# Residual projections taken by column halves, and the weight splits, banks and convolution parts that follow, in a two-block transformer kernel

## The chip, the cores and the metric

The kernel runs on one core of a Trainium2 chip. The metric is the device time of one execution in microseconds (us), the median of three runs. Smaller is better. TensorE (PE) multiplies, VectorE (DVE), ScalarE (ACT) and GpSimd (POOL) work elementwise, SyncE (SP) issues the transfers.

## The reference, cut to what matters

256 tokens of width 1024 pass through two blocks. The first has four token mixers and an MLP with squared ReLU; the second has block attention with rotary embedding, a causal depthwise convolution of 31 taps, and a gated MLP. Both blocks share one skeleton, in which the changed code lies:

```python
h = rms_norm(x, mix_norm_g)
ys, gate_logit = _token_mixers(h, w_in, ...)
x = x + jnp.sum(gates * branch, axis=2) @ w_out       # "wo"
h = rms_norm(x, mlp_norm_g)
x = x + jnp.square(jax.nn.relu(h @ w_up)) @ w_down    # "up", "dn"
x = rms_norm(x, final_norm_g)
h = rms_norm_2(x, norm1_g)
proj = h @ w_in_2                                     # "p2": q, k, v, u
attn = moba_attention(rope(norm(q)), rope(norm(k)), v)
conv = conformer_conv(u, glu_b, dw_w, dw_b, ln_g, ln_b)
x = x + jnp.concatenate([attn, conv], axis=-1) @ w_out_2   # "wo2"
h = rms_norm_2(x, norm2_g)
x = x + (silu(h @ w_gate) * (h @ w_up_2)) @ w_down_2       # "g", "u", "d2"
```

## The kernel before

**Products.** Every large product is made in float32 precision by three passes of rounded operands: a weight `w` becomes `whi` (rounded, a cast on ScalarE, `split_hi`, L998) and `wlo = w - whi` (VectorE, `split_lo`, L1403), and an activation likewise `Ahi/Alo`, `Bhi/Blo`, `hhi/hlo` (L1012, L1417). `product` (L536 to L538) multiplies hi by hi, hi by lo and lo by hi for up to four blocks of 128 rows, so a product of 512 columns is 12 matmuls. A product is named by a tag such as `("up", j, ui, t)`: `t` is the half of the tokens (0 or 1), `ui` the half of the contraction, `n` the half of the output columns.

**Weight units.** Weights arrive in units of 1 MB (512 rows by 512 columns). Each unit serves two products, one for each `t`. SyncE loads units into four `raw` buffers; a load waits until both splits of the unit four before are done. The split results live in three slots (`NSPL = 3`), so unit i may be split only when the last product of unit i-3 is done.

**Order.** There is no scheduler at run time: each engine has a fixed list, and semaphores hold it where it must wait. TensorE's order of products is `groups`. ScalarE and VectorE call `after(tag)` and `before(tag)` at the place of each product in their own lists; these issue the split of unit i+2 at the last product of unit i (`ends`). Whatever stands behind a waiting instruction in a list waits too.

**The joints.** Where a residual is followed by a normalisation, the order is special. The last four products of "wo", "dn" and "wo2" go (t, n) = (0,0), (0,1), (1,0), (1,1). Each adds to the residual `xr` on VectorE (`residual`, L1659), is transposed by TensorE (`turn_res`, into bank 5+n), scaled by the gain (`gained`, `x_gain` L1423) and split (L1012, L1417); ScalarE squares it (L1151) for the norm. The first chunk of the next stage goes in `FIRST` order, (ui, t) = (0,0), (1,0), (0,1), (1,1), and all later chunks in `PLAIN` order, (0,0), (0,1), (1,0), (1,1). `W_ACC` gives the accumulators of (t, n): banks 3, 4, 7, 0. The first chunks of "p2" use banks 0 and 1, so the first one waits for the residual that empties bank 0.

**Behind "p2".** Each chunk of "p2" is evacuated by `evac2` (L1248), which for the first chunk waits for two inverse roots (`stats2`: four squares "F" of `xr` times a gain that GpSimd multiplies in at L1972). Then come the rotary work (`r0`, `ra`, `r1` on VectorE, L1764 to L1793, turned by `rturn`), and a loop over ten steps k with eight attention heads (`az` scores, `at` transposition, `ap` times V, `aw` evacuation at L1293/L1294), between which TensorE makes 16 parts of the convolution (`conv`, L845), two in each of the first eight steps. `ln_turn`, `ln`, `ln_back` and `ln_silu` are the convolution's LayerNorm and swish, placed among the first four "wo2" products.

Of the kernel before, what the change touches and what calls it, by code (L numbers as in the profile page):

```python
# [17 lines left out]
NPC = 2  # L18
# [53 lines left out]


# [90 lines left out]
def build(nc, ctx, x_d, w_in, w_br, w_out, w_up, w_dn, w_in2, w_out2, w_g2, w_u2, w_d2, par_d, par2_d, cst_d, tw_d, out_d):  # L164
# [143 lines left out]
    def plan_out(name, src):  # L308
# [4 lines left out]
        for t in range(2):  # L313
            for n in range(2):
                group(u[1][n], name, 1, n, t)

    def plan_down(name, src, j, kn, last):
        if kn == 4:
            u = [add_unit(src, 4 * j, 4, 512 * n, 512) for n in range(2)]
            for n, t in ([(n, t) for t in range(2) for n in range(2)] if last else PLAIN):  # L320
                group(u[n], name, j, n, t)
# [5 lines left out]
    def plan_up(name, src, j, n, first):  # L327
        u = [add_unit(src, 4 * k, 4, 512 * j, n) for k in range(2)]
        for ui, t in (FIRST if first else PLAIN):
            group(u[ui], name, j, ui, t)  # L330

    plan_out("wo", w_out)
    for j in range(8):
        plan_up("up", w_up, j, 512, j == 0)
        if j:
            plan_down("dn", w_dn, j - 1, 4, False)
    plan_down("dn", w_dn, 7, 4, True)
    for i, (c0, n) in enumerate(CH2):
        u = [add_unit(w_in2, 4 * k, 4, c0, n) for k in range(2)]
        for ui, t in (FIRST if i == 0 else PLAIN):  # L340
            group(u[ui], "p2", i, ui, t)
    plan_out("wo2", w_out2)
    for j in range(6):
        plan_up("g", w_g2, j, HC2[j] * 128, j == 0)
        plan_up("u", w_u2, j, HC2[j] * 128, False)
        if j:
            plan_down("d2", w_d2, j - 1, HC2[j - 1], False)
    plan_down("d2", w_d2, 5, 2, True)

    nu = len(units)  # L350

    free_at = {}
    ends = {}
    for tag, i in unit_of.items():
        free_at[i] = groups[tag] + 1
    for i, g in free_at.items():
        ends[g - 1] = i
# [10 lines left out]
    for key in [("A", t, h) for t in range(2) for h in range(2)] + [("B", t, h) for h in range(2) for t in range(2)] \  # L368
            + [("M", t, h) for h in range(2) for t in range(2)] + [("N1", t, n) for t in range(2) for n in range(2)] \
            + [("H", j, t) for j in range(8) for t in range(2)] + [("N2", t, n) for t in range(2) for n in range(2)] \  # L370
            + [("Y", t, h) for h in range(3) for t in range(2)] + [("N3", t, n) for t in range(2) for n in range(2)] \
# [7 lines left out]
    SQ = {key: i for i, key in enumerate([("x", t) for t in range(2)] + [(k, t, n) for k in ("N1",) for t in range(2)  # L379
                                                                       for n in range(2)]  # L380
                                         + [("N2", t, n) for t in range(2) for n in range(2)]
                                         + [("F", t, n) for t in range(2) for n in range(2)]
                                         + [("N3", t, n) for t in range(2) for n in range(2)])}
# [110 lines left out]
    def _(e):  # L494
# [261 lines left out]
        def turn_res(name, t, n):  # L756
            key = (name, t, n)
            base = {"N1": 0, "N2": 4, "N3": 8}[name]
            w.wait_ge(s_res, base + 2 * t + n + 1)
# [13 lines left out]
        for t in range(2):  # L773
            for n in range(2):
                bk = W_ACC[t, n]
                w.wait_ge(s_xl, X["M", t, 1] + 1)
                product(("wo", 1, n, t), Ahi, Alo, 4, t, lambda c0, bk=bk: bank[bk], False, True)
                gone[bk] = (s_res, 2 * t + n + 1)
                if (t, n) != (0, 0):
                    turn_res("N1", *((0, 0), (0, 1), (1, 0))[2 * t + n - 1])  # L780

        def up(name, j, src, hi, lo, first, tail=None):
            for q, (ui, t) in enumerate(FIRST if first else PLAIN):
# [9 lines left out]
        def down(name, j, key, last, tail=None):  # L793
            hi, lo = hhi[:, j % 2], hlo[:, j % 2]
            for k, (n, t) in enumerate([(n, t) for t in range(2) for n in range(2)] if last else PLAIN):
# [5 lines left out]
                if last:  # L801
                    gone[bk] = (s_res, 4 + 2 * t + n + 1)
# [6 lines left out]
        for j in range(8):  # L809
            up("up", j, "N1", Bhi, Blo, j == 0, (lambda: turn_res("N1", 1, 1)) if j == 0 else None)  # L810
# [6 lines left out]
        down("dn", 7, "H", True, lambda k: k and turn_res("N2", *((0, 0), (0, 1), (1, 0))[k - 1]))  # L817
# [53 lines left out]
        def ap(h):  # L871
            w.wait_ge(s_ev, 36 + 10)
            w.wait_ge(s_ac, h + 1)
            clear(2)
            P, v = PT2[:, h % 2, :], V2[:, :, 64 * h:64 * h + 64]
            e.matmul(bank[2][:, 0:64], P[:, 0:128], v[:, 0, :], start=True, stop=True)
            e.matmul(bank[2][:, 64:128], P[:, 128:256], v[:, 0, :], start=True, stop=False)
            e.matmul(bank[2][:, 64:128], P[:, 256:384], v[:, 1, :], start=False, stop=True).then_inc(s_ap, 1)
            gone[2] = (s_aw, h + 1)
# [21 lines left out]
        gone[0], gone[1] = (s_ev, 45), (s_ev, 46)  # L901
        for k in range(10):
            if k < 8:
                az(k)
                conv(2 * k)
            if 1 <= k < 9:
                at(k - 1)
            if k < 8:
                conv(2 * k + 1)
            if k > 1:  # L910
                ap(k - 2)
        for t in range(2):
# [3 lines left out]
            turn_x(key, ys[:, t, 0:512])  # L916

# [32 lines left out]
        for t in range(2):  # L950
            for n in range(2):
                bk = W_ACC[t, n]
                product(("wo2", 1, n, t), Bhi, Blo, 4, t, lambda c0, bk=bk: bank[bk], False, True,
                        at={0: (s_xl, X["Y", t, 1] + 1), 2: (s_xl, X["Y", t, 2] + 1)})
                gone[bk] = (s_res, 8 + 2 * t + n + 1)
                if (t, n) != (0, 0):
                    turn_res("N3", *((0, 0), (0, 1), (1, 0))[2 * t + n - 1])


        for j in range(6):  # L960
            nk = HC2[j]
            up("g", j, "N3", Ahi, Alo, j == 0, (lambda: turn_res("N3", 1, 1)) if j == 0 else None)
            gone[1], gone[2] = (s_sg, 2 * j + 1), (s_sg, 2 * j + 2)
            up("u", j, None, Ahi, Alo, False)
# [13 lines left out]
    def _(e):  # L978
# [175 lines left out]
        def norm_turn(name, t, n, o):  # L1154
            base = {"N1": 0, "N3": 8}[name]
            w.wait_ge(s_res, base + 2 * t + n + 1)
# [12 lines left out]
        def out_proj(name, norm, o):  # L1169
# [8 lines left out]
            for t in range(2):  # L1178
                for n in range(2):
                    after(name, 1, n, t)  # L1180
                    if (t, n) != (0, 0):
                        p = ((0, 0), (0, 1), (1, 0))[2 * t + n - 1]
                        norm_turn(norm, *p, o)
                        gained((norm, *p))

        out_proj("wo", "N1", o2)

        def plain_order(first):
            return FIRST if first else PLAIN
# [12 lines left out]
        for j in range(8):  # L1202
            for q, (ui, t) in enumerate(plain_order(j == 0)):
                after("up", j, ui, t)
# [3 lines left out]
                if q == (2 if j == 0 else 3):  # L1208
                    relu2(j, 0)
            if j:  # L1210
                for k, (n, t) in enumerate(PLAIN):
                    after("dn", j - 1, n, t)
# [866 lines left out]
```

## Time and profile before

| | |
|---|---|
| median of 3 runs | 847.89 us (847.79 to 848.2) |
| the profiled execution | 847.93 us |
| its span, first to last instruction | 846.1 us |
| TensorE busy | 807.1 us (95%) |
| VectorE, ScalarE, GpSimd busy | 467.6, 406.5, 33.9 us |
| mean granted TensorE clock | 0.991 |

The span is the time from the first to the last recorded instruction; about 1.8 us of the execution lie outside it. TensorE's matmuls overlap: a record of 0.39 us starts every 0.227 us, so the end that the profile draws lies 0.16 us behind the start of what may follow. An idle time in brackets is counted from that drawn end.

### The profile page before, as it was taken

The page shows a single profiled execution, that of the slowest core. Times are in us where ns is not written, and L with a number is a line of the kernel's source. Part 1 is how long each engine was busy: PE and PEld are TensorE (multiplying, and loading weights), DVE is VectorE, ACT ScalarE, POOL GpSimd, SP SyncE. Part 2 cuts the span into 40 slices and gives each one's busy share as a digit, 9 for nine tenths or more (in the row PEclk, how much of TensorE's full clock was granted, in tenths as well). Part 3 has the DMA queues.
Part 4 walks back from the last instruction along what each step waited for, and adds up shares of the span by engine and source line. Part 5 has one row for each costly group of instructions (what it writes and reads, how often), then busy time and mean ns, then how long its engine had stood idle before and what let it go on. Part 6 is the DMA issues. An engine that isn't in the chain of part 4 may idle for free.

```text
span 846.1 us, 9700 instructions
## 1 busy us (share of the span) xinstructions
PE 807.1 (95%) x3930; PEld 663.6 (78%) x3930; DVE 467.6 (55%) x616; ACT 406.5 (48%) x539; POOL 33.9 (4%) x33
## 2 busy tenths in 40 slices
PE   6999999999999898999999998999998999999997
PEld 4887888877778686888888876877876788888896
DVE  5445354556756865454444447688735555444543
ACT  6554454454546626555454436454435443344341
POOL 0000000000000410000000003020000000000000
PEclk9999999999999999999999999999989999999999
DMA  9742424333446364555555546644112654654441
GB/s 336 284 150 76 149 75 149 119 138 142 147 153 195 110 225 151 197 173 181 195 193 184 177 144 241 214 149 149 51 49 71 229 184 142 224 196 149 140 159 50
DMA packets 68268, 136.25 MB, mean 161 GB/s; under 512 B 2304, under 2 KB 7040, under 8 KB 67584
## 3 DMA queue, kind: packets, MB, share of 16 engines
q1 hardware_dynamic: 67760, 134.44, 46.5%
q10 hardware_dynamic: 464, 1.20, 0.4%
q8 instruction: 31, 0.51, 0.2%
q14 instruction: 13, 0.11, 0.0%
HBM read 134.43 MB, written 1.05 MB: 160 GB/s over the span
## 4 chain that ended last, share of the span: by engine, by line
PE 87%; DVE 6%; ACT 3%; issue 2%; POOL 1%; DMA 1%; ACTq 0%; SPq 0%; DVEq 0%
PE b L536 19%; PE b L538 18%; PE b L537 18%; PE SS L536 4%; PE SS L538 4%; PE SS L537 4%; PE TT L505 3%; DVE wlo L1403 2%; PE OO L536 2%; PE OO L537 2%; PE OO L538 2%; PE OO L845 2%; PE SS L621 1%; PE b L680 1%; DMA xr<-in_x 1%
## 5 line engine op out<-in xcount | busy, mean ns | idle before, releaser
L1403 DVE TENSOR_TENSOR wlo<-raw,whi 128x2048 fp32r<-128x2048 f32 (+2 forms) x123 | 271.7, 2217 | 103.6 <-ACT whi L998 103.6
L998 ACT CAST whi<-raw 128x2048 fp32r<-128x2048 f32 (+2 forms) x123 | 227.5, 1850 | 124.5 <-PE b L538 93.2
L536 PE MATMUL b<-whi,Ahi 128*128 128x512 f32 (+2 forms) x568 | 222.2, 391 | 9.0 <-DVE wlo L1403 3.7
L538 PE MATMUL b<-whi,Alo 128*128 128x512 f32 (+2 forms) x568 | 216.1, 381 | 0.0
L537 PE MATMUL b<-wlo,Ahi 128*128 128x512 f32 (+2 forms) x568 | 215.5, 379 | 0.0
L536 PEld LDWEIGHTS b<-whi,Ahi 128*128 128x128 f32 x568 | 107.7, 190 | 32.3 <-issue 8.1
L538 PEld LDWEIGHTS b<-whi,Alo 128*128 128x128 f32 x568 | 107.4, 189 | 20.9
L537 PEld LDWEIGHTS b<-wlo,Ahi 128*128 128x128 f32 x568 | 107.9, 190 | 18.4
L536 PE MATMUL b<-whi,Bhi 128*128 128x512 f32 x168 | 66.7, 397 | 5.5 <-DVE wlo L1403 2.8
L1417 DVE TENSOR_TENSOR hlo<-TT,hhi 128x512 fp32r<-128x512 f32 (+1 forms) x28 | 17.7, 668 | 91.3 <-ACT hhi L1012 91.3
L538 PE MATMUL b<-whi,Blo 128*128 128x512 f32 x168 | 65.5, 390 | 0.0
L537 PE MATMUL b<-wlo,Bhi 128*128 128x512 f32 x168 | 65.5, 390 | 0.0
L536 PE MATMUL SS<-whi,hhi 128*128 128x512 f32 x108 | 42.4, 392 | 1.7 <-DVE hlo L1417 1.7
L1012 ACT CAST hhi<-TT 128x512 fp32r<-128x512 f32 (+1 forms) x28 | 14.8, 573 | 57.8 <-PE TT L505 57.8
L538 PE MATMUL SS<-whi,hlo 128*128 128x512 f32 x108 | 42.1, 389 | 0.0
L537 PE MATMUL SS<-wlo,hhi 128*128 128x512 f32 x108 | 42.0, 389 | 0.0
L536 PEld LDWEIGHTS b<-whi,Bhi 128*128 128x128 f32 x168 | 31.5, 188 | 12.7 <-DVE gates L1640 3.4
L538 PEld LDWEIGHTS b<-whi,Blo 128*128 128x128 f32 x168 | 31.5, 188 | 6.7
L537 PEld LDWEIGHTS b<-wlo,Bhi 128*128 128x128 f32 x168 | 31.6, 188 | 6.1
L1947 POOL TENSOR_TENSOR st<-st 128x2 f32<-128x2 f32 (+3 forms) x13 | 15.4, 1183 | 414.6 <-DVE st L1427 414.6
L1084 ACT ACTIVATE Sb<-Sb,st 128x384 f32<-128x384 f32 (+3 forms) x16 | 9.9, 617 | 39.2 <-DVE st L1522 39.2
L536 PEld LDWEIGHTS SS<-whi,hhi 128*128 128x128 f32 x108 | 20.3, 188 | 6.3 <-DVE hlo L1417 2.2
(264 smaller groups left out, 999.7 us busy)
## 6 DMA issues: line engine op xcount, KB each, us to landing
raw<-in_w_in SPq DMA_DIRECT2D x42, 1024.0 KB, 4.9
raw<-in_w_up SPq DMA_DIRECT2D x16, 1024.0 KB, 5.4
raw<-in_w_dn SPq DMA_DIRECT2D x16, 1024.0 KB, 7.2
raw<-in_w_d SPq DMA_DIRECT2D x11, 1024.0 KB, 5.0
raw<-in_w_g SPq DMA_DIRECT2D x10, 1024.0 KB, 5.3
raw<-in_w_u SPq DMA_DIRECT2D x10, 1024.0 KB, 4.9
raw<-in_w_out SPq DMA_DIRECT2D x8, 1024.0 KB, 5.0
raw<-in_w_br SPq DMA_DIRECT2D x4, 1024.0 KB, 5.1
```

Source lines behind the costliest of these rows:

```text
L505: ins = e.transpose(dst[:, 128 * k:128 * k + 128], src[:, 128 * k:128 * k + 128], ident)
L536: e.matmul(dst, xh, H[:, kc, c0:ce], start=first and kc == krs[0], stop=False)
L537: e.matmul(dst, xh, L[:, kc, c0:ce], start=False, stop=False)
L538: ins = e.matmul(dst, xl, H[:, kc, c0:ce], start=False, stop=last and kc == krs[-1])
L621: ins = e.matmul(SS[:, m * g:m * g + m], qkA[p:p + 64, q, qs], qkA[p:p + 64, k, 0:m], start=True, stop=True)
L845: ins = e.matmul(bank[7][:, 128 * i:128 * i + 128], tw[:, i % 3, 128 * j:128 * j + 128], hp[:, i, j:j + 128], start=j == 0, stop=j == NSH - 1)
L998: e.copy(whi[:, s, 0:m], raw[:, r, 0:m]).then_inc(s_hi, 1)
L1012: e.copy(ph, src).then_inc(s_xh, 1)
L1084: ins = e.activation(P, P, ACT.Exp, bias=stat_m[i][:, 0:1], accum_out=stat_s[i][:, 0:1])
L1403: e.tensor_tensor(wlo[:, s, 0:m], raw[:, r, 0:m], whi[:, s, 0:m].bitcast(F32), ALU.subtract).then_inc(s_lo, 1)
L1417: e.tensor_tensor(pl, src, ph.bitcast(F32), ALU.subtract).then_inc(s_xl, 1)
L1947: e.tensor_tensor(r, v, mhalf[:, 0:n], ALU.pow).then_inc(s_rs, 1)
```

## The change

All four-product ends of residual projections go by column halves: `ORD` gives (t, n) = (0,0), (1,0), (0,1), (1,1), so that a weight unit's two products are neighbours. The first chunks of "up", "p2" and "g" go in `PLAIN` order as all others. The turned residuals go to bank 5+t. "p2" uses banks 1 and 2 in place of 0 and 1, and `ap` bank 0 in place of 2. From the first residual's last four products on, unit i is split at the place of the product just behind the last one of unit i-3, one place earlier than before; up to there the places stay. At the joints, calls of `after` and `before` now stand behind the residual's and the gain's work. The convolution's parts are spread otherwise over the attention loop: two in steps 0 to 3, one in steps 4 to 9, one behind the loop and one behind the turns of the attention's result.

```diff
+ORD = [(0, 0), (1, 0), (0, 1), (1, 1)]
...
-    bg[2] += [("gt", 0)]
-    bg[3] += [("gs", 0)]
-    bg[4] += [("gt", 1)]
+    bg[3] += [("gt", 0)]
+    bg[4] += [("gs", 0), ("gt", 1)]
...
+    turn = groups["wo", 1, 0, 0]
+    split_after = {}
+    for i in range(NPC, nu):
+        g = free_at[i - 2] - 1
+        if g >= turn:
+            g = free_at[i - NSPL]
+        assert g not in split_after, (g, i)
+        split_after[g] = i
...
-        xbank[key] = {"A": (3 if a else 5) + n, "M": 5 + a, "N1": 5 + n, "N2": 5 + n, "N3": 5 + n, "H": 5 + n,
+        xbank[key] = {"A": (3 if a else 5) + n, "M": 5 + a, "N1": 5 + a, "N2": 5 + a, "N3": 5 + a, "H": 5 + n,
...
-            clear(2)
+            clear(0)
...
-        gone[0], gone[1] = gone[W_ACC[1, 1]], (s_up, 15)
         for i in range(5):
-            for q, (ui, t) in enumerate(FIRST if i == 0 else PLAIN):
+            for q, (ui, t) in enumerate(PLAIN):
                 w.wait_ge(s_xl, X["N2", t, ui] + 1)
                 if ui == 0 and i == 0:
-                    clear(t)
+                    clear(1 + t)
...
-                product(("p2", i, ui, t), Ahi, Alo, 4 * ui, t, lambda c0, t=t: bank[t], ui == 0, ui == 1)
+                product(("p2", i, ui, t), Ahi, Alo, 4 * ui, t, lambda c0, t=t: bank[1 + t], ui == 0, ui == 1)
...
         for k in range(10):
             if k < 8:
                 az(k)
-                conv(2 * k)
+                tile_part()
             if 1 <= k < 9:
                 at(k - 1)
-            if k < 8:
-                conv(2 * k + 1)
+            if k < 4 or k > 7:
+                tile_part()
             if k > 1:
                 ap(k - 2)
+        tile_part()
...
+        tile_part()
...
-            i = ends.get(groups[tag])
-            if i is not None and i + 2 < nu:
-                split_hi(i + 2)
+            if groups[tag] in split_after:
+                split_hi(split_after[groups[tag]])
...
-            i = ends.get(groups[tag] - 1)
-            if i is not None and i + 2 < nu:
-                split_lo(i + 2)
+            i = split_after.get(groups[tag] - 1)
+            if i is not None and i > split_done[0]:
+                split_lo(i)
+                split_done[0] = i
...
-                if q == (2 if i == 0 else 3):
+                if q == 3:
                     evac2(i, 0)
+                after("p2", i, ui, t)
...
-            for t in range(2):
-                for n in range(2):
-                    before(name, 1, n, t)
-                    w.wait_ge(s_mm, done(name, 1, n, t))
-                    residual(base, t, n)
-                    if (t, n) != (0, 0):
-                        p = ((0, 0), (0, 1), (1, 0))[2 * t + n - 1]
-                        gained((norm, *p), pcol(gain, 4 * p[1], 4))
+            for k, (t, n) in enumerate(ORD):
+                w.wait_ge(s_mm, done(name, 1, n, t))
+                residual(base, t, n)
+                if k:
+                    p = ORD[k - 1]
+                    gained((norm, *p), pcol(gain, 4 * p[1], 4))
+                before(name, 1, n, t)
```

## Rows read from the trace of the kernel before

**Rows 1.** The page: busy time, share of the span, instructions of TensorE
```profile
PE 807.1 (95%) x3930; PEld 663.6 (78%) x3930; DVE 467.6 (55%) x616; ACT 406.5 (48%) x539; POOL 33.9 (4%) x33
```
**Rows 2.** Waits of TensorE: us in total, times, longest
```profile
PE b L536 <- DVE wlo L1403: 6.5, 6, 1.4
```
**Rows 3.** Timeline of TensorE, first residual into "up": start, us, what [idle before]
```profile
323.39 0.47 PE L536 MATMUL b<-whi,Bhi 128*128 128x512 f32 x1 [1.42 <-DVE wlo L1403]
...
328.17 0.47 PE L536 MATMUL b<-whi,Bhi 128*128 128x512 f32 x1 [1.33 <-DVE wlo L1403]
...
338.01 0.66 PE L505 MATMUL TT<-cst,ust 128*128 128x128 f32 x4 [1.00 <-ACT ust L1200]
```
**Rows 4.** The page's costliest groups: the two splits; busy, mean ns | idle before
```profile
L1403 DVE TENSOR_TENSOR wlo<-raw,whi 128x2048 fp32r<-128x2048 f32 (+2 forms) x123 | 271.7, 2217 | 103.6 <-ACT whi L998 103.6
L998 ACT CAST whi<-raw 128x2048 fp32r<-128x2048 f32 (+2 forms) x123 | 227.5, 1850 | 124.5 <-PE b L538 93.2
```
**Rows 5.** Timeline of TensorE from the second residual into "p2"
```profile
513.40 0.47 PE L536 MATMUL b<-whi,Ahi 128*128 128x512 f32 x1 [2.39 <-DVE xr L1659]
...
525.38 0.66 PE L505 MATMUL TT<-cst,ys 128*128 128x128 f32 x4 [1.49 <-ACT ys L1248]
...
528.62 0.39 PE L536 MATMUL b<-whi,Ahi 128*128 128x512 f32 x1
```
**Rows 6.** Stretches: us, busy of PE, PEld, DVE, ACT, POOL, PEclk, DMA share, GB/s
```profile
513.40:518.17 4.77, 4.77 (x16) 3.81 (x17) 3.39 (x3) 1.24 (x3) 0.43 (x1) 0.64 0.73 220
...
617.57:623.21 5.64, 5.64 (x14) 4.37 (x15) 1.14 (x2) 2.89 (x2) 0.00 (x0) 0.51 0.00 0
...
700.34:711.22 10.88, 10.88 (x49) 8.96 (x48) 3.38 (x3) 3.82 (x2) 0.00 (x0) 1.00 0.58 193
```
**Rows 7.** Timeline of ScalarE: the first evacuation of "p2"
```profile
524.64 0.69 ACT L1248 ACTIVATE ys<-b,st 128x512 f32<-128x512 f32 x1 [0.51 <-DVE st L1759]
```
**Rows 8.** Timelines of VectorE and GpSimd where both read SBUF
```profile
509.39 1.11 DVE L1417 TENSOR_TENSOR Alo<-tg,Ahi 128x512 fp32r<-128x512 f32 x1 [0.69 <-ACT Ahi L1012]
...
511.87 1.97 POOL L1972 TENSOR_TENSOR xr<-xr,par 128x512 f32<-128x512 f32 x1 [1.92 <-ACT ys L1151]
...
518.56 1.30 POOL L1972 TENSOR_TENSOR xr<-xr,par 128x512 f32<-128x512 f32 x1 [4.73 <-PE TT L505]
```
**Rows 9.** The rotary stretch, columns as in rows 6
```profile
549.10:578.59 29.49, 27.44 (x125) 21.55 (x124) 25.86 (x39) 16.89 (x20) 8.06 (x4) 1.00 0.46 153
```
**Rows 10.** Timeline of TensorE: the third turn of the rotary work
```profile
574.06 0.66 PE L505 MATMUL TT<-cst,PT 128*128 128x128 f32 x4 [0.39 <-DVE PT L1793]
```
**Rows 11.** Timelines in the attention loop: convolution parts, taps on VectorE
```profile
604.51 1.11 PE L845 MATMUL OO<-hp,tw 128*128 128x128 f32 x8
...
608.85 1.10 PE L845 MATMUL OO<-hp,tw 128*128 128x128 f32 x8
...
600.99 2.84 DVE L1831 SCALAR_TENSOR_TENSOR ca<-ch,par,ca 128x256 f32<-128x256 f32 x7
```
**Rows 12.** Timeline of TensorE: the loop's end into "wo2"
```profile
614.04 0.41 PE L876 MATMUL b<-V,PT 128*128 128x64 f32 x2 [0.70 <-ACT ys L1294]
...
615.51 1.25 PE L505 MATMUL TT<-cst,ys 128*128 128x128 f32 x8 [0.61 <-ACT ys L1294]
...
617.57 0.79 PE L536 MATMUL SS<-whi,Bhi 128*128 128x512 f32 x1 [0.81 <-DVE Blo L1417]
```
**Rows 13.** Timeline of TensorE: the third residual into "g" and "u"
```profile
640.32 0.79 PE L536 MATMUL OO<-whi,Bhi 128*128 128x512 f32 x1 [2.32 <-DVE wlo L1403]
...
653.12 0.47 PE L536 MATMUL b<-whi,Ahi 128*128 128x512 f32 x1 [1.41 <-DVE wlo L1403]
...
657.89 0.47 PE L536 MATMUL b<-whi,Ahi 128*128 128x512 f32 x1 [1.33 <-DVE wlo L1403]
...
666.14 0.39 PE L536 MATMUL b<-whi,Ahi 128*128 128x512 f32 x1
```
**Rows 14.** DMA issues: count, KB each, median us to landing
```profile
raw<-in_w_dn SPq DMA_DIRECT2D x16, 1024.0 KB, 7.2
```

More of the change, by code:

```diff
@@ L312, in plan_out, with plan_down @@
                 group(u[0][n], name, 0, n, t)
-        for t in range(2):
-            for n in range(2):
-                group(u[1][n], name, 1, n, t)
-    def plan_down(name, src, j, kn, last):
+        for n, t in PLAIN:
+            group(u[1][n], name, 1, n, t)
+    def plan_down(name, src, j, kn):
         if kn == 4:
             u = [add_unit(src, 4 * j, 4, 512 * n, 512) for n in range(2)]
-            for n, t in ([(n, t) for t in range(2) for n in range(2)] if last else PLAIN):
+            for n, t in PLAIN:
                 group(u[n], name, j, n, t)
@@ L325, in plan_down, with plan_up @@
                 group(u, name, j, 0, t)
-    def plan_up(name, src, j, n, first):
+    def plan_up(name, src, j, n):
         u = [add_unit(src, 4 * k, 4, 512 * j, n) for k in range(2)]
-        for ui, t in (FIRST if first else PLAIN):
+        for ui, t in PLAIN:
             group(u[ui], name, j, ui, t)
@@ L772, in _, with up @@
                         turn_x(("M", t_, 1), ys[:, t_, 512:1024])
[L773 to L778, printed above, removed]
-                if (t, n) != (0, 0):
-                    turn_res("N1", *((0, 0), (0, 1), (1, 0))[2 * t + n - 1])
-        def up(name, j, src, hi, lo, first, tail=None):
-            for q, (ui, t) in enumerate(FIRST if first else PLAIN):
+        for k, (t, n) in enumerate(ORD):
+            bk = W_ACC[t, n]
+            w.wait_ge(s_xl, X["M", t, 1] + 1)
+            product(("wo", 1, n, t), Ahi, Alo, 4, t, lambda c0, bk=bk: bank[bk], False, True)
+            gone[bk] = (s_res, k + 1)
+            if k:
+                turn_res("N1", *ORD[k - 1])
+        def up(name, j, src, hi, lo, tail=None):
+            for q, (ui, t) in enumerate(PLAIN):
                 bk = 1 + t
@@ L794, in down @@
             hi, lo = hhi[:, j % 2], hlo[:, j % 2]
-            for k, (n, t) in enumerate([(n, t) for t in range(2) for n in range(2)] if last else PLAIN):
+            for k, (n, t) in enumerate(PLAIN):
                 bk = W_ACC[t, n]
@@ L1177, in out_proj @@
                         ln_silu()
[L1178 to L1181, printed above, removed]
-                        p = ((0, 0), (0, 1), (1, 0))[2 * t + n - 1]
-                        norm_turn(norm, *p, o)
-                        gained((norm, *p))
+            for k, (t, n) in enumerate(ORD):
+                if k:
+                    norm_turn(norm, *ORD[k - 1], o)
+                    gained((norm, *ORD[k - 1]))
+                after(name, 1, n, t)
         out_proj("wo", "N1", o2)
-        def plain_order(first):
-            return FIRST if first else PLAIN
         def relu2(j, t):
@@ L1202, in _ @@
         for j in range(8):
-            for q, (ui, t) in enumerate(plain_order(j == 0)):
-                after("up", j, ui, t)
+            for q, (ui, t) in enumerate(PLAIN):
                 if j == 0 and q == 0:
@@ L1360, in _ @@
         for j in range(6):
-            for q, (ui, t) in enumerate(plain_order(j == 0)):
-                after("g", j, ui, t)
+            for q, (ui, t) in enumerate(PLAIN):
                 if j == 0 and q == 0:
@@ L1734, in _ @@
         w.wait_ge(s_sq, SQ["N1", 1, 1] + 1)
-        for k, (t, n) in enumerate(PLAIN):
-            before("dn", 7, n, t)
+        for k, (t, n) in enumerate(ORD):
             w.wait_ge(s_mm, done("dn", 7, n, t))
@@ L1739, in _ @@
             if k:
-                turn2(*PLAIN[k - 1])
+                turn2(*ORD[k - 1])
+            before("dn", 7, n, t)
         def stats2():
@@ L1894, in ln @@
                                 ALU.mult).then_inc(s_lv, 1)
-        ends.pop(groups["wo2", 0, 0, 0] - 1, None)
         w.wait_ge(s_dve, k_x)
@@ L1911, in _ @@
         for j in range(6):
[L1912 removed]
+            for q, (ui, t) in enumerate(PLAIN):
                 before("g", j, ui, t)
```

135 lines of the change are left out of this document (66 added, 69 removed).

## The prediction

> **What bounds the kernel.** I read the page first. TensorE is busy 95% of the span [rows 1], so little but its 39 us of idle time, and stretches at a lower clock, can be won. I then read TensorE's waits: the largest entry is the low half of a split weight, six waits, 6.5 us together [rows 2]. Last I read the timeline of all engines around every wait over 0.3 us. The reader is to see that most of the avoidable ones lie at the three joints where a residual product meets the next stage [rows 3, 5, 13] and at the end of the attention loop [rows 12]. In between nothing waits: four products of 12 matmuls take 10.88 us at clock 1.00 [rows 6], 2.72 us each, with a turn of 0.35 us here and there. A product that starts after a wait costs some 0.13 us more than its place in a running row (it refills), so a wait of 1.42 us costs about 1.55.
>
> The clock is the second thing to read. The product that starts after the 2.39 us wait [rows 5] runs in a stretch with a mean granted clock of 0.64 [rows 6], that is, partly at 1.2 in place of 2.4 GHz; the stretch takes 4.77 us where product and turn need 3.2, so the drop costs 1.5. After the 2.32 us wait the first matmul shows 0.79 us instead of 0.47 [rows 13]: the same drop and price. The first "wo2" product comes after 2.5 us of small waits, has clock 0.51 and takes 5.64 us with the turn behind it [rows 6, 12], 2.4 too much. The wait of 1.49 us [rows 5] and those of 1.4 us [rows 3] are followed by matmuls at full clock.
>
> **First joint, wo into up: 2.2 us won.** Before, the two weight units of the last four products, and then the two of the first chunk, are used in turns, so a unit is released only with the third product of four. Its slot's next split (1.9 us on ScalarE, 2.3 on VectorE [rows 4]) then has two products, 5.4 us, and shares the lists with residuals and gains; the first and the second product of "up" wait 1.42 and 1.33 us for it [rows 3]. By column halves a unit is released after two products, and the next one in its slot is wanted four products later. The first product's split is done ahead, and the second product uses the same unit: both waits go, 3.0 us with the refills. What is late next is the third product: its low half stands on VectorE behind residual and gain of the fourth product (three operations of 0.7 and a cast of 0.6 us, then 2.3 for the split). Followed operation by operation it ends 0.4 us after TensorE arrives: 0.5 us comes back. In `PLAIN` order the t = 0 half of the chunk is complete one product later, so its squared ReLU is done late, when TensorE is already there; the second half queues behind it on ScalarE, where one wait of 1.00 us was [rows 3]: 0.3 us comes back. 3.0 - 0.5 - 0.3 = 2.2. Bounds: 3.0 if both hide, 1.2 if a cast more stands in front.
>
> **Middle of both MLPs: nothing.** ScalarE's order there is the same instruction by instruction, because the calls move one product earlier but behind the evacuation that they used to precede. On VectorE one split per step now stands ahead of the hidden layer's split instead of behind it; it is ready within 4.2 us (1.9 + 2.3 [rows 4]) of a release that lies 5.4 us ahead of the turn, so the products in between cover it. Without that cover it would cost up to 2.3 us in each of 14 steps.
>
> **Second joint, dn into p2: 2.4 us won, of which 0.9 arrives.** The first "p2" product no longer waits for the residual that empties bank 0: 2.39 us and the 1.5 us of low clock go [rows 5, 6]. But the first evacuation bounds what follows, since the second chunk needs its bank. Before, it starts at 524.64 [rows 7], with one cast of a split between the squares and it. Now two casts are in front of it in ScalarE's list, since it stands at the fourth product and not at the third: 1.9 us more, less the 0.5 it waited for the root [rows 7] and some 0.9 by which the squares start earlier. It starts 0.5 us later, at about 525.2. But then all four products are already made, where one was still to follow (2.8 us with the refill). The second chunk starts 1.05 us after the evacuation's start (0.69, and 0.35 for the turn), at 526.2 against 528.62 [rows 5]: 2.4 won, with a new wait of about 2.3 us in front of the turn. Among this stands a collision: an operation of VectorE whose inputs both lie in SBUF took 1.11 instead of 0.69 us when GpSimd was multiplying, and GpSimd's took 1.97 instead of 1.30 when VectorE was splitting [rows 8]. The splits now fall on those products; I have put 0.8 us for it.
>
> Behind it the rotary work is VectorE's: 25.9 of 29.5 us busy [rows 9], and TensorE's third turn waits for it [rows 10]. The new places put a fourth weight split (2.3 us) ahead of that turn where three stood, while the first of these no longer has to stand behind the first rotary group; that one in turn waits for a cast that is held by the second GLU operation, itself now behind a split. Adding the list up (four splits 9.1, four rotary groups of about 2.85, the scalings and taps 3.1), the third turn comes 0.9 us earlier than 574.06 and TensorE stands 2.5 us or so in front of it. So 0.9 of the 2.4 us reaches the attention loop. Bounds: 2.4 if VectorE keeps up, -0.5 if the collision costs a whole split twice.
>
> **New waits and the clock: 1.5 us lost.** There are now two waits, of about 2.3 and 2.5 us. Waits of 2.39 and 2.32 us were followed by the lower level, those of 1.49 were not [rows 5, 6, 13]. I take one drop of 1.5 us, between none and two (3.0).
>
> **Attention loop: 2.9 us won.** The loop's step takes 4.33 us from one convolution part to the next of its kind [rows 11], TensorE always busy. A part costs 0.89. With one part less in steps 4 to 7 a step needs 3.44 us of TensorE, and VectorE needs about the same (seven taps 2.84 [rows 11] and 0.65 of small operations), so the four steps shrink by 3.6. The four parts come back at the end, where TensorE waited 0.37, 0.70, 0.61 and 0.81 us [the last three: rows 12] for the eighth head's evacuations and the split of the turned result: 2.5 and some 0.4 of refills. The rest of the parts' time stays: the gain is what they fill, 2.9. If VectorE's list does not shrink, 2.0; the low clock afterwards is counted below.
>
> **Third joint, wo2 into g: 9.1 us won.** The loop's end is now dense, so I expect the first "wo2" product at full clock: 2.4. The split of the fourth unit is cast ahead of the swish, so the 2.32 us wait goes with its refill (2.5) and its low clock (1.5) [rows 13]. The two waits at the start of "g", 1.41 and 1.33 [rows 13], go as at the first joint (3.0 with refills), and 0.3 to 0.5 come back at the third product. 2.4 + 2.5 + 1.5 + 3.0 - 0.4 = 9.0; with the operation by operation reckoning 9.1. The first "u" product, at 666.14 before, needs the first silu, which is done just in time. Bounds: 9.5, and 6.7 if the "wo2" product stays slow.
>
> **Banks.** The turns alternate between banks 5 and 6 in either numbering. The Trainium skill (TensorE: Matmul & The Clock Gate, "A second HAM failure mode: psum-queue depth-cycling") tells of a kernel that cycles through PSUM banks between groups, whose clock swings between the two levels for it; the new order 3, 4, 7, 0 would by that pay a drop at each of the three joints, 4.5 us in all: 838.8. The down products already run in that order, at clock 1.00 [rows 6], so it is nothing by the row.
>
> **The sum.** 2.2 + 0.9 - 1.5 + 2.9 + 9.1 = 13.6. The profiled execution took 847.93 us (span 846.1 and 1.8 around it), 0.04 from the median: 847.9 - 13.6 = 834.3 us.
>
> **Rivals.** (a) No new drop of the clock: both waits are new and their lengths are uncertain by 0.5 us, so they may fall nearer 1.5; 832.8 us, 831.5 if the bounds above help too. Chance 0.22. (b) The second block's projections give back more: both waits bring the lower clock (835.8), and the collision is the full one. The mechanism is that of the collision above [rows 8]: GpSimd's fourth multiplication, 1.3 us, slips between the small split and the weight split in VectorE's list, and everything up to the third turn is 1.3 later: 837.1 with both. Chance 0.24. The Trainium skill (SBUF — State Buffer, "SBUF: two separate sides") says that VectorE with two SBUF inputs and GpSimd lock each other out for a whole instruction; by that rule, the trace agrees, since both were longer [rows 8]. (c) The end of the loop stays sparse enough for a slow "wo2" product, or VectorE bounds steps 4 to 7: 2.4 to 4 us less won, 836.7 to 838.3, and to 846 with several such. Chance 0.09. (d) The other side: splits are placed one product earlier in lists that are strictly in order, ahead of evacuations. If a unit's transfer has not landed, ScalarE stands, the evacuation stands, and TensorE with it. A 1 MB transfer lands 7.2 us after issue in the slowest group [rows 14]; a raw buffer is reloaded about 17 us ahead of its cast (four units of 5.44 us less 4.2 for the split). ScalarE's waits before its casts are for TensorE [rows 4]. It decides once transfers land more than 17 us after issue; to lose 13.6 us over 14 MLP steps they must be 18 us: 848.5. Chance 0.02, and 0.01 for no difference. The forecast keeps 0.42.
>
> **Numbers.** Likeliest 834.3. Leaving out less than 2 in 10, the range reaches from 831.2 (case a with its bounds) to 838.2 (b, and most of c). 0.2% is 1.7 us, about what a measurement here can tell from none: faster 0.97, same 0.01, slower 0.02.
>
> **What the profile after would show.** No wait for L1403 at the first two products of "up" and "g", but one of up to 0.5 us at the third. The first "p2" product starts directly behind a turn, at full clock; a wait of 2 to 2.5 us for the evacuation L1248 in front of the first GLU turn, and one as long for the rotary scaling L1793 in front of the third rotary turn, with a low clock behind one of them. Attention steps 4 to 7 of 3.4 to 3.5 us. The first "wo2" product in 2.8 and not 5.3 us, and none waiting for a split there. The time from the first residual's last product to the joint in p2 unchanged but for 2.2 us. The prediction is wrong if the evacuation before the first GLU turn is later than I followed it, if the clock drops elsewhere, or if casts start to wait for DMA.

## The result and the profile after

The changed kernel took 835.06 us (median of 4 runs, 833.48 to 835.67), beside 847.93 us (847.79 to 848.2) for the kernel before on the same chip: 12.9 us less, ratio 0.9845 with a 95% interval of 0.9828 to 0.9862. The forecast was 834.3 us, range 831.2 to 838.2. The profiled execution is the fastest of the four, 833.48 us; its span is 831.6 us (846.1 before), its mean granted clock 0.999 (0.991 before). The other three executions (834.89 to 835.67 us) have a mean clock of 0.995.

The page of the profile after, the row that answers to [rows 1]:
```profile
PE 801.0 (96%) x3930; PEld 659.9 (79%) x3930; DVE 470.7 (57%) x616; ACT 405.2 (49%) x539; POOL 34.6 (4%) x33
```
TensorE is busy 6.1 us less with the same 3930 instructions: mostly the lower clock that has gone. The other 8.4 of the 14.5 us of span are idle time, 39.0 before and 30.6 now.

Waits first. The timeline of TensorE after, from the first residual into "up" [rows 3], then from the second residual to the attention loop [rows 5, 10]:
```profile
329.11 0.47 PE L542 MATMUL b<-whi,Bhi 128*128 128x512 f32 x1
...
335.14 0.66 PE L511 MATMUL TT<-cst,ust 128*128 128x128 f32 x4 [0.32 <-ACT ust L1205]
...
336.38 0.66 PE L511 MATMUL TT<-cst,ust 128*128 128x128 f32 x4 [0.58 <-ACT ust L1205]
...
509.08 0.48 PE L542 MATMUL b<-whi,Ahi 128*128 128x512 f32 x1
...
517.03 0.47 PE L542 MATMUL b<-whi,Ahi 128*128 128x512 f32 x1 [1.74 <-DVE wlo L1407]
...
524.84 0.66 PE L511 MATMUL TT<-cst,ys 128*128 128x128 f32 x4 [2.09 <-ACT ys L1253]
...
572.37 0.66 PE L511 MATMUL TT<-cst,PT 128*128 128x128 f32 x4 [2.66 <-DVE PT L1799]
```
At the first joint the waits of 1.42 and 1.33 us are gone, and the third product (329.11) has no idle time in brackets. Its weight split on VectorE ends at 328.96, just as TensorE comes for it:
```profile
326.68 2.28 DVE L1407 TENSOR_TENSOR wlo<-raw,whi 128x2048 fp32r<-128x2048 f32 x1
```
At the second joint the first "p2" product starts right behind a turn (509.08), the third waits 1.74 us for a weight split, and the two new waits of the forecast stand where it put them, 2.09 and 2.66 us long. Behind neither does the clock fall in this execution: the stretch behind the first one (first row below) has clock 1.00. The stretches of the timeline, columns as in [rows 6]; the second is two steps of the attention loop, the third the first "wo2" product up to the turn behind it [rows 12], the fourth the start of "g" to the first "u" product [rows 13]:
```profile
524.84:528.11 3.27, 3.27 (x17) 2.71 (x17) 3.27 (x3) 3.27 (x6) 0.00 (x0) 1.00 0.99 413
596.13:603.01 6.88, 6.88 (x47) 5.70 (x46) 6.88 (x21) 3.50 (x15) 0.00 (x0) 1.00 0.39 145
612.72:615.59 2.87, 2.87 (x12) 2.31 (x13) 2.46 (x3) 1.51 (x1) 0.00 (x0) 1.00 0.00 0
639.95:651.69 11.74, 11.74 (x56) 9.41 (x54) 8.93 (x11) 8.54 (x11) 0.70 (x1) 1.00 0.49 173
```
The steps take 3.44 us (4.33 before). The "wo2" product takes 2.87 us at full clock, where it took 5.28 to that turn's start. "g" has no wait left in its first four products, where two stood. Between the first "wo2" product and "g" one wait over 0.3 us is left, for the low half of an activation; the kernel before has it too (0.43 us):
```profile
628.95 0.50 PE L542 MATMUL SS<-whi,Bhi 128*128 128x512 f32 x1 [0.45 <-DVE Blo L1424]
```

**Where the time went.** From the start of one named product to that of another, before and after. Across the profiles of the kernels below, such stretches agree within 0.1 us where a kernel's code and its clock are the same, so they tell more than whole times do.

| stretch | before | after | won | forecast |
|---|---|---|---|---|
| kernel start to the last four products of "wo" (code unchanged) | 309.52 | 310.66 | -1.14 | 0 |
| "wo", last four products, to the first of the second chunk of "up" | 28.91 | 26.13 | 2.78 | 2.2 |
| from there to the last four "dn" products | | | 0.0 | 0 |
| last four "dn" products to the second chunk of "p2" | 30.26 | 28.55 | 1.71 | 2.4 |
| from there to the first score product of the attention loop | 49.97 | 51.66 | -1.69 | -1.5 |
| the loop, to the first "wo2" product | 38.98 | 35.81 | 3.17 | 2.9 |
| first "wo2" product to the first "u" product | 48.57 | 38.97 | 9.60 | 9.1 |
| new drops of the clock | | | 0 here | -1.5 |

The sum, 14.5, is the difference of the spans. The first row is put down to chance. The code up to there is unchanged, and the nine profiles taken with the changed code alone spread over 2.3 us at this place. Both kernels run their first products at half speed, the matmuls 0.43 us apart, and the full speed comes at 15.45 us before and at 18.02 after. Ten profiles reach "wo" at ten different times (last part).

Why the third "p2" product waits is seen where VectorE and GpSimd read SBUF together. VectorE's timeline, then GpSimd's, after [beside rows 8]:
```profile
512.22 1.37 DVE L1424 TENSOR_TENSOR Alo<-tg,Ahi 128x512 fp32r<-128x512 f32 x1 [1.06 <-ACT Ahi L1022]
513.51 3.37 DVE L1407 TENSOR_TENSOR wlo<-raw,whi 128x2048 fp32r<-128x2048 f32 x1
...
511.75 2.99 POOL L1976 TENSOR_TENSOR xr<-xr,par 128x512 f32<-128x512 f32 x2 [3.21 <-ACT ys L1161]
```
Two GpSimd multiplications run back to back from 511.75 to 514.74. The small split takes 1.37 instead of 0.69 us and the weight split 3.37 instead of 2.28: 0.68 + 1.09 = 1.77 us. The forecast had put 0.8 for this.

The first evacuations of "p2" on ScalarE, after [beside rows 7]:
```profile
524.11 1.25 ACT L1253 ACTIVATE ys<-b,st 128x512 f32<-128x512 f32 x2
```
Counted from the last four "dn" products, the first evacuation starts at 27.4 us, and at 26.3 us before: 1.1 us later, where the forecast had 0.5. A later evacuation than it had followed was one of the signs that it named for being wrong.

### The profile page after: what moved, and what is told of

It reads as the page before. It is cut to its first block, busy times and chain, and to the rows that moved or that the text cites. A ratio compares the mean times of both kernels' runs of the same rounds, so it can differ in the third digit from the quotient of the medians.

```text
span 831.6 us, 9701 instructions
## 1 busy us (share of the span) xinstructions
PE 801.0 (96%) x3930; PEld 659.9 (79%) x3930; DVE 470.7 (57%) x616; ACT 405.2 (49%) x539; POOL 34.6 (4%) x33
## 4 chain that ended last, share of the span: by engine, by line
PE 85%; DVE 7%; ACT 3%; issue 2%; DMA 1%; POOL 1%; ACTq 0%; SPq 0%; DVEq 0%
PE b L542 19%; PE b L544 18%; PE b L543 18%; PE SS L542 4%; PE SS L544 4%; PE SS L543 4%; PE TT L511 3%; DVE wlo L1407 3%; PE OO L542 2%; PE OO L544 2%; PE OO L543 2%; PE OO L850 2%; ACT whi L1009 1%; PE SS L627 1%; PE b L686 1%
```

## The experiments

Each kernel is the changed one with the edit shown. Those of the first group ran beside the kernel before at 848.5 us (845.56 to 851.64, 11 runs), those of the second group beside it at 848.12 (846.45 to 848.78, 9 runs). Single executions of one kernel differ by up to 6 us, so the traces carry the argument and the times only bound it. "Joint" is the stretch from the last four "dn" products to the first GLU turn (28.14 after), "rotary" that from this turn to the first score product (52.07 after).

**1. The convolution's parts as before.**
```diff
-            if k < 4 or k > 7:
+            if k < 8:
                 tile_part()
...
-        tile_part()
```
(both single calls behind the loop go)

> The changed kernel with the convolution's parts spread as before: two in each of steps 0 to 7. Theory A (the parts fill the waits at the loop's end and keep the clock up for the first wo2 product): the stretch from the first scores to the first wo2 product grows by 3.2 us back to 39.0, the waits of 0.4, 0.7, 0.6 and 0.8 us come back, and the first wo2 product runs at the low clock again, 2.4 us more: 835.1 + 5.6 = 840.7 us. Rival B (the clock there has another cause): 3.2 us more only, 838.3. Rival C (VectorE bounds the loop): under 1 us, 836 or less.

Measured: 839.72 us (837.61 to 842.7, 6 runs), ratio 0.9902 [0.9876, 0.9927]. The timeline of TensorE at the loop's end, then three stretches of this kernel: around the first "wo2" product, this product itself, and the stretch behind the first GLU turn:
```profile
614.40 0.41 PE L881 MATMUL b<-V,PT 128*128 128x64 f32 x2 [0.70 <-ACT ys L1297]
...
615.86 1.09 PE L511 MATMUL TT<-cst,ys 128*128 128x128 f32 x8 [0.61 <-ACT ys L1297]
...
617.91 0.80 PE L542 MATMUL SS<-whi,Bhi 128*128 128x512 f32 x1 [0.96 <-DVE Blo L1422]
```
```profile
616.50:624.00 7.50, 6.54 (x23) 5.04 (x20) 4.18 (x4) 2.87 (x3) 0.00 (x0) 0.54 0.14 28
617.91:623.20 5.29, 5.29 (x12) 4.03 (x13) 3.44 (x3) 1.51 (x1) 0.00 (x0) 0.50 0.10 12
523.94:528.12 4.18, 4.18 (x14) 3.35 (x15) 4.18 (x3) 3.34 (x6) 0.00 (x0) 0.60 0.98 408
```
The small waits come back as they were [rows 12], and with them the low clock of the first "wo2" product. The loop takes 38.97 us (+3.16) and the product 5.29 (+2.42), together the 5.6 us that were expected of this run; the forecast had 2.9 and 2.4 for the two. So a step that the forecast only assumed is seen: behind waits of 0.4 to 1.0 us in a thin stretch the clock is low, and with parts that exist anyway in their place it stays up, in all eight profiles that have the new places. It does not fall so far every time, though. In the profiled execution the mean clock is 0.54 over 7.5 us here (first row of the stretches), so it is low for 6.9 us, which takes 0.004 off the mean of the whole execution. Two of the six executions (837.8 and 838.15 us) have a mean clock of 0.998, so in those this drop was missing or shorter, and their times are near rival B's 838.3. The three with 0.991 or 0.992 took 841.29 to 842.7 us. The profiled execution has two drops more, both at the new waits of the second block (the last row, clock 0.60, and the same at 573.0).

**2. The weight splits at their old places everywhere.**
```diff
-        if g >= turn:
+        if g >= turn and False:
             g = free_at[i - NSPL]
```


> The changed kernel with every weight split at its old place, one product later, and all orders, banks and parts new. Theory A (the order by column halves carries the gain, the earlier places only move it about): the first products of up, p2 and g wait some 1.7 to 2 us each for their low half, 5.3 together, but the first evacuation of p2 comes 1.4 us earlier and the rotary stretch needs one split less ahead of its third turn, 1.7: 835.1 + 5.3 - 3.1 = 837.3 us, between 835.5 and 839. The wait of 2.3 us in wo2 stays away. Rival B (the early places carry it): the wait in wo2 and both low clocks come back, 841 us or more. Rival C (places don't matter): 835.

Measured: 835.55 us (835.24 to 837.25, 5 runs), ratio 0.9855 [0.9834, 0.9876]. The timeline of TensorE:
```profile
324.95 0.47 PE L542 MATMUL b<-whi,Bhi 128*128 128x512 f32 x1 [1.41 <-DVE wlo L1407]
...
513.02 0.47 PE L542 MATMUL b<-whi,Ahi 128*128 128x512 f32 x1 [1.85 <-DVE wlo L1407]
...
525.63 0.66 PE L511 MATMUL TT<-cst,ys 128*128 128x128 f32 x4 [0.90 <-ACT ys L1253]
...
572.91 0.66 PE L511 MATMUL TT<-cst,PT 128*128 128x128 f32 x4 [0.40 <-DVE PT L1799]
...
642.23 0.47 PE L542 MATMUL b<-whi,Ahi 128*128 128x512 f32 x1 [1.42 <-DVE wlo L1407]
```
One wait of 1.4 us comes back at the start of "up" (the first joint's stretch is 1.48 us longer) and one at that of "g" (1.55 longer up to the first "u" product). The second wait at each place, and the one of 2.3 us inside "wo2", stay away: the old places do not bring them back, so they went by the new orders. In the second block the old places are better: the joint takes 27.11 us (-1.03) though its first product waits 1.85, and rotary 51.83 (-0.24), because neither the evacuation nor the third rotary turn stands behind an early split. Net 1.8 us in the trace. The waits that the first theory foretold are there, 4.7 us of them and not 5.3, and the time lies at the lower edge of its range, near that of the third theory, since the second block gives so much back. So the earlier places pay at the first and third joint and cost at the second.

**3. "p2" on its old banks.**
```diff
-                    clear(1 + t)
+                    clear(t)
...
-                product(("p2", i, ui, t), ..., lambda c0, t=t: bank[1 + t], ui == 0, ui == 1)
+                product(("p2", i, ui, t), ..., lambda c0, t=t: bank[t], ui == 0, ui == 1)
```
(`ap` on bank 2 again; the evacuations and the lines on when a bank is free likewise)

> The changed kernel with p2 on banks 0 and 1 and the attention's last product on bank 2, as before. Theory A (in the new order the third product of p2 waits for its weight split anyway, so what the first one loses is taken out of that wait): the first p2 product starts 1.6 us later, the third at the same time, the sum moves by 0.3 us at most: 835.1 to 835.4 us. Rival B (the bank carries the second joint's gain): 1.6 us later all along, and a lower clock behind it: 836.7 to 838.2 us.

Measured: 834.41 us (830.87 to 835.23, 6 runs), ratio 0.983 [0.9806, 0.9853]. The timelines of TensorE, VectorE and GpSimd:
```profile
511.79 0.47 PE L542 MATMUL b<-whi,Ahi 128*128 128x512 f32 x1 [1.33 <-DVE Alo L1425]
...
524.88 0.66 PE L511 MATMUL TT<-cst,ys 128*128 128x128 f32 x4 [1.47 <-ACT ys L1254]
...
511.01 0.68 DVE L1667 TENSOR_TENSOR xr<-xr,b 128x512 f32<-128x512 f32 x1
...
514.64 2.28 DVE L1408 TENSOR_TENSOR wlo<-raw,whi 128x2048 fp32r<-128x2048 f32 x1
...
512.87 1.29 POOL L1977 TENSOR_TENSOR xr<-xr,par 128x512 f32<-128x512 f32 x1 [3.21 <-ACT ys L1162]
515.36 2.71 POOL L1977 TENSOR_TENSOR xr<-xr,par 128x512 f32<-128x512 f32 x1 [1.20 <-PE TT L511]
```
Neither theory holds. The first product waits 1.33 us. The view names the small split, but that had ended at 511.09; what ends at 511.69 and empties bank 0 is the residual L1667. And yet the joint takes 27.05, 1.09 us less than with the new banks. The last quarter's turn stands behind that product, so it comes later, and GpSimd's multiplication of this quarter starts at 515.36, inside VectorE's split and not ahead of it. Now GpSimd is the one that stretches (2.71), which nobody waits for, and the split takes its 2.28. The wait of 1.33 lies where TensorE would have waited for that split anyway. The profiled execution has a drop behind the third rotary turn (rotary 53.63).

**4. Hardly any GpSimd work there.** GpSimd multiplies 16 of the 512 columns of each quarter; the final gain is left out of the other 496.
```diff
-            e.tensor_tensor(xs, xs, par2[:, 512 * n:512 * n + 512], ALU.mult)
+            e.tensor_tensor(xs[:, 0:16], xs[:, 0:16], par2[:, 512 * n:512 * n + 16], ALU.mult)
```


> The changed kernel with GpSimd's four multiplications by the final gain cut to 16 of 512 columns each, so that the rest of that gain is left out. Theory A (VectorE's split stood still while GpSimd multiplied): the split that ends before the third p2 product takes 2.3 and not 3.4 us, the product's wait of 1.7 us falls to about 0.3, the first evacuation and all up to the rotary work come 1.3 us earlier: 833.8 us. Rival B (that split is long for another reason, or the evacuation is bound by ScalarE's casts alone): 835.0 us, with the split at 3.4 us or the evacuation where it was.

Measured: 832.89 us (829.85 to 835.87, 6 runs), ratio 0.982 [0.9793, 0.9847]. VectorE's timeline, then GpSimd's:
```profile
512.39 0.69 DVE L1424 TENSOR_TENSOR Alo<-tg,Ahi 128x512 fp32r<-128x512 f32 x1 [1.06 <-ACT Ahi L1022]
513.00 2.28 DVE L1407 TENSOR_TENSOR wlo<-raw,whi 128x2048 fp32r<-128x2048 f32 x1
...
511.92 0.22 POOL L1976 TENSOR_TENSOR xr<-xr,par 128x16 f32<-128x16 f32 x1 [4.28 <-ACT ys L1161]
513.05 2.31 POOL L1976 TENSOR_TENSOR xr<-xr,par 128x16 f32<-128x16 f32 x1 [0.91 <-ACT ys L1161]
```
Both splits have their own durations again, the wait at the third product is gone, and the joint takes 26.37: 1.77 us less, just the 0.68 + 1.09 that the two had been longer. The third turn still waits 2.68 us, so all 1.77 arrive at the attention loop, but for a drop of the clock behind the first GLU turn (+1.57 in rotary).

**5 and 6. Old places in "p2" alone; the same with the old banks.**
```diff
             g = free_at[i - NSPL]
+        if groups["p2", 0, 0, 0] <= g < groups["wo2", 0, 0, 0]:
+            g = free_at[i - 2] - 1
```


> The changed kernel, but from the first p2 product to the first wo2 product each weight unit is split at the places of before (one product later than in the changed kernel). Theory A (the earlier places are what stands in front of the first evacuation and of the rotary work): the first evacuation of p2 comes 1.3 to 1.4 us earlier, the wait of 2.09 us in front of the first GLU turn shrinks below 1, the third rotary turn waits less than 2 us, the stretch from the first p2 product to the first score product is 1 to 2 us shorter, 832 us. Theory B (the splits come too late there, as in the run with the old places everywhere, which waited 1.85 us at the first p2 product): that wait returns because the slot is free late, and the time stays at 834 to 836 us.

> The changed kernel with the places of the run before this one in p2, and p2 on banks 0 and 1 (ap on 2) as before the change. Theory A (the old banks keep GpSimd's multiplications out of VectorE's splits, and the old places free ScalarE for the evacuation; the two add): 1.1 us less than the run with the places alone, about 831 us. Theory B (both relieve the same wait, that in front of the first GLU turn, so they don't add): the same as the places alone within 0.4 us by the intervals of the trace, because the evacuation is then bounded by the inverse root.

Measured: places alone 832.32 us (831.89 to 833.35, 5 runs), ratio 0.9822 [0.9808, 0.9837]; with the banks 830.5 (829.5 to 831.86, 4 runs), ratio 0.9799 [0.9783, 0.9815]. The timeline of TensorE with the places alone, then with both:
```profile
517.34 0.47 PE L544 MATMUL b<-whi,Ahi 128*128 128x512 f32 x1 [1.74 <-DVE wlo L1409]
523.96 0.66 PE L513 MATMUL TT<-cst,ys 128*128 128x128 f32 x4 [0.93 <-ACT ys L1255]
...
571.25 0.66 PE L513 MATMUL TT<-cst,PT 128*128 128x128 f32 x4 [0.39 <-DVE PT L1801]
```
```profile
511.53 0.47 PE L544 MATMUL b<-whi,Ahi 128*128 128x512 f32 x1 [1.34 <-DVE Alo L1427]
...
524.84 0.50 PE L544 MATMUL b<-whi,Ahi 128*128 128x512 f32 x1 [0.76 <-DVE wlo L1410]
```
Places alone: the joint 26.92 (-1.22), rotary 51.84 (-0.23), the long waits cut to 0.93 and 0.39. The wait of 1.74 stays, so it was never one for the place. With the late places a wait of 0.8 us for a weight split stands in front of the second chunk (last row, and as long in the other kernel). With the banks: the joint 25.81, another 1.11 less, rotary 51.86. The two add, as the first theory said. The last kernel beats both kernels of the comparison: 17.6 us under before and 3.0 under run 7, the changed kernel measured beside it. Of the 3.0, 2.5 are in the trace. The rest is likely the drops, since no wait over 1.4 us is left there, but this is argued and not shown. Three of its four runs have a mean clock of 1.0; the profiled one has 0.997, with a stretch of lower clock at 116 to 119 us, in the first block.

**7. The changed kernel again.** No edit.

> The changed kernel again, for one more profile of it. Theory A (its two waits of 2.1 and 2.7 us bring the lower clock in some executions and not in others): the stretches between joints repeat within 0.1 us except behind these two waits, where one or both are 1.5 us longer; 833.5 to 837 us. Theory B (the lower clock comes from something else in the disturbed profiles): both waits again without a drop, and the spread of 833.5 to 835.7 us lies elsewhere, such as at the kernel's start.

Measured: 833.49 us (832.98 to 835.44, 4 runs), ratio 0.9837 [0.9821, 0.9854]. The profiled execution is the slowest of them. Its timeline, and the stretches behind the two waits:
```profile
524.02 0.66 PE L511 MATMUL TT<-cst,ys 128*128 128x128 f32 x4 [2.10 <-ACT ys L1253]
...
573.12 1.12 PE L511 MATMUL TT<-cst,PT 128*128 128x128 f32 x4 [2.67 <-DVE PT L1799]
```
```profile
524.02:528.20 4.18, 4.18 (x14) 3.35 (x15) 4.18 (x3) 3.34 (x6) 0.00 (x0) 0.59 0.99 403
573.12:576.70 3.58, 3.58 (x12) 3.06 (x13) 2.74 (x2) 1.18 (x2) 0.00 (x0) 0.61 0.84 273
```
Waits of the same length as in the first profile, and this time the clock falls behind both: rotary takes 54.93 instead of 52.07, 2.86 more. All other stretches repeat within 0.05 us, and the start differs by 0.75. The first theory holds. The other three executions have mean clocks of 0.997 to 0.999 and take 832.98 to 833.58 us.

**8. The waits filled with transposes of a constant into a free bank.**
```diff
+                    if i == 0:
+                        fill(5)     # 20 transposes, ahead of the first GLU turn
...
+                    if i == 2:
+                        fill(6)     # 24, ahead of the third rotary turn
```


> The changed kernel with transposes of a constant into a free bank, about 1.1 to 1.3 us of them in front of the first GLU turn and as many in front of the third rotary turn, where TensorE waits 2.1 and 2.7 us; they add work only inside the waits. Theory A (the idle time of these waits is what lowers the clock): no stretch behind them is at a lower clock, the executions lie closer together, 833 to 834 us. Theory B (the clock falls for another reason, or the transposes delay the turns): drops as often as without them, or both stretches longer by what the transposes take beyond the wait; 834 to 836 us.

Measured: 833.88 us (831.93 to 834.83, 4 runs), ratio 0.9835 [0.9817, 0.9852]. The timeline of TensorE:
```profile
523.94 2.34 PE L889 MATMUL b<-cst 128*128 128x128 f32 x20
526.21 0.66 PE L511 MATMUL TT<-cst,ys 128*128 128x128 f32 x4
...
570.90 2.78 PE L889 MATMUL b<-cst 128*128 128x128 f32 x24
573.73 0.66 PE L511 MATMUL TT<-cst,PT 128*128 128x128 f32 x4
```
The transposes took 2.34 and 2.78 us, twice what was expected, and so fill the waits from end to end. Both stretches are as long as in the first profile, joint 28.10 and rotary 52.07, with no drop behind them (the one of this profile lies at 116 to 120 us, in the first block), and the mean clock is 0.998 or 1.0 in all four runs (0.995 in four of the changed kernel's eight). So idle time is most likely what lowers the clock there; without the transposes six of nine such waits had a drop, and only two filled ones were profiled. The time, however, is not better than that of run 7, and the runs lie no closer together: that half of the expectation failed. The profiled execution reaches "wo" 2.2 us later than that of run 7, by the code ahead of it, which is the same; this offsets most of the 2.86.

## Why the prediction came out as it did

**First joint, 2.2 forecast, 2.78 measured.** The mechanism is right: both waits gone, which is the 3.0 of the forecast, and the squared ReLU a little late (0.32 and 0.58, answering to 1.00), which takes back 0.1 and not 0.3. The mis-sized term is the 0.5 that should come back at the third product: its low half was ready at 328.96, as TensorE got there, and 0.1 us came back. Run 2 splits the gain: 1.48 are the earlier places, and the rest is put down to the orders by subtraction. No run puts the orders back alone.

**Middle of the MLPs, nothing.** Right to 0.05 us. No cast waited for a transfer, so rival (d) found nothing to stand on.

**Second joint, 2.4 forecast of which 0.9 arrives; 1.71, and nothing arrives.** The new waits came where they were put (2.09 for 2.3, 2.66 for 2.5), and the rotary list gave back 1.69 for 1.5. The mis-sized term is the collision: 0.8 for 1.77 us. This is the mechanism of rival (b), which had GpSimd's fourth multiplication slip in between the two splits and priced it at 1.3 us more. The row that the 0.8 was sized by [rows 8] showed one operation stretched by 0.4; the new order puts two of GpSimd's multiplications back to back ahead of a weight split, and the split waits for the whole of what is left. Run 4 shows it: without this work 1.77 us come back and all arrive. That GpSimd starts so early is itself part of the change, since the first "p2" product no longer holds back the last quarter's turn: the new banks remove a wait of 1.33 us (not the 2.39 of before, which the new order of residuals had already shortened, and behind which no drop was left) and cost 2.4 (runs 3 and 6). The forecast counted the removed wait and not this. The Trainium skill (SBUF — State Buffer, "SBUF: two separate sides") says that a VectorE operation with two SBUF inputs and a GpSimd operation that reads SBUF exclude each other for the whole instruction. The trace agrees on either side: the split of 3.37 us ends 2.14 us behind the multiplications, which is nearly its whole own duration, and the multiplication of 16 columns took 2.31 us beside a split of 2.28.

**The clock, one drop of 1.5 forecast.** The size is right (1.4 to 1.6 us each), the number a matter of chance: none in the first profile, two in run 7. Over all profiles, nine waits of 2.09 to 2.68 us stood in front of these turns; the clock fell behind six. Those of 1.85 us and less were not followed by a drop there. By the mean clocks of the changed kernel's eight runs (0.995 four times, 0.997 once, 0.999 three times) an average of about one drop is likely; this is argued from the two profiled ones, 0.999 with none and 0.995 with two, and not seen in the others. Rival (a) was the first profile. Run 7's profile is rival (b), with both drops and the full collision, at 835.44 and not 837.1 us because the first and third joint and the loop won more than forecast.

**Attention loop 2.9, third joint 9.1; 3.17 and 9.60 measured.** Every step came as followed: 3.44 us a step, the "wo2" product at full clock, no weight split waited for. Run 1 confirms the first two together. At the third joint 0.1 of the 0.3 to 0.5 for the third product came, as at the first. Of the 9.60, run 1 gives 2.4 to the clock of the "wo2" product and run 2 gives 1.55 to the earlier places; the rest, the wait of 2.32 us with its drop above all, goes to the new orders by subtraction.

**Banks.** That a cycle 3, 4, 7, 0 with 1 and 2 behind it costs no clock is right: no drop at the first and third joint in any of the nine profiles that have it. But "nothing" was wrong for another reason, the 1.1 us of run 3.

**The sum.** The steps without the clock came to 15.1, and were 15.6 in the trace; the start took back 1.1. The errors of the steps (+0.6, -0.9, +0.3, +0.5) cancel in part, and so do the start and the drops, which are chance. That the total came within 0.8 us is partly luck.

## What to carry to other kernels

A product that may start earlier also lets its followers start earlier: list what the released work runs beside, above all VectorE and GpSimd reading SBUF together, and price the whole remaining instruction, not a share. One rule for where weights are split suited two joints and hurt the third; where the same list also carries evacuations on the critical path, a split one place later was worth 1.5 us. Waits of over 2 us in front of TensorE cost the clock on top, not always but more often than not, so shortening such a wait (those of 1.85 us and less had no drop in a dense stretch here), or moving real work into it, pays twice.

## What the runs showed of the hardware

- The drop behind a wait is not fixed by its length: a wait of 2.09 us had none in one execution and 1.57 us of low clock in another; waits of 2.64 to 2.68 us had none twice and a drop three times.
- The first block differs by chance: the same instructions reach the first "wo" product between 297.7 and 300.3 us in ten profiles. The first matmuls are 0.43 us apart and later 0.23, though the granted clock of the stretch is given as 1.00; the full speed came at 15.45 us in one profile and at 18.02 in another, worth 1.2 us, and four of the ten profiles have a stretch of lower clock between there and "wo". A comparison of stretches between named products is free of it.
- GpSimd's multiplication of 16 columns took 0.22 us alone and 2.31 us beside a VectorE split (run 4).
- Small waits can cost as much clock as one long one: behind waits of 0.36, 0.70, 0.61 and 0.96 us among small matmuls the clock was low for 6.9 us (run 1), and by their mean clocks two of the six executions did not have this, or had less of it.
